# The last output weight of a feed-forward, loaded, rounded and split in two halves

## The reference, cut to what matters

```python
x = _ln(ALPHA * x + 0.5 * _swiglu(x, f_in[1], f_out[1]), g[2], b[2])   # D_MODEL 1024, D_FF 2816, 544 tokens, fp32
```

## Time and profile before

| | |
|---|---|
| median of 3 runs | 2879.94 us (2871.91 to 2883.61) |
| the profiled execution | 2882.67 us, span of its trace 2881.1 us |
| TensorE (PE) busy | 2669.0 us, 93% of the span |
| VectorE (DVE) / ScalarE (ACT) / GpSimd (POOL) busy | 1019.4 / 764.9 / 345.2 us |
| the second feed-forward's output products | 1277 to 1426 us in layer 0, 2704 to 2851 us in layer 1 |

### The profile page before, as it was taken

One profiled execution on the slowest core, in us unless ns is written; L12 is line 12 of the kernel. 1 busy time (PEld: TensorE's weight loads), 2 busy tenths in 40 slices (PEclk: granted clock), 3 DMA queues, 4 the chain that ended last, 5 costly groups with the idle time before them and its releaser, 6 DMA issues.

```text
span 2881.1 us, 49666 instructions
## 1 busy us (share of the span) xinstructions
PE 2669.0 (93%) x18108; PEld 2385.0 (83%) x18108; DVE 1019.4 (35%) x1876; ACT 764.9 (27%) x1167; POOL 345.2 (12%) x321
## 2 busy tenths in 40 slices
PE   7999999998888899999899999999988888999996
PEld 7999788896456899999899987888954568999995
DVE  2222121535553632241532211224456437222415
ACT  2222000421342332231232210014213424222313
POOL 0000000024231200013100000001242311000240
PEclk9999999997985999999999999999957859999998
DMA  3222543113421122222122234321153301222222
GB/s 138 86 86 88 155 138 110 55 61 131 139 81 58 59 74 87 87 84 90 62 88 87 87 115 146 128 90 61 46 172 112 86 33 59 88 87 87 90 81 81
DMA packets 110003, 265.86 MB, mean 92 GB/s; under 512 B 15347, under 2 KB 85138, under 8 KB 90770
## 3 DMA queue, kind: packets, MB, share of 16 engines
q1 hardware_dynamic: 99778, 233.21, 23.9%
q0 software_dynamic: 10080, 30.73, 3.3%
HBM read 258.15 MB, written 14.24 MB: 95 GB/s over the span
## 4 chain that ended last, share of the span: by engine, by line
PE 51%; issue 36%; DVE 4%; POOL 3%; DMA 1%; ACT 1%; DVEq 1%; POOLq 1%; SPq 1%; PEldq 0%; PEld 0%; ACTq 0%
PE PS L462 50%; POOL wo_lo L393 2%; POOL wi_lo L451 1%; DVEq L1429 1%; SPq L319 1%; PE PS L952 1%; DMA WO<-wo_dram 1%; POOLq L402 1%; DVE xs L1547 0%; DVE sm L1893 0%; ACT WO L1118 0%; POOLq L406 0%; DVE Z L1432 0%; DMA WI<-wi_dram 0%; DVE WO L1432 0%
## 5 line engine op out<-in xcount | busy, mean ns | idle before, releaser
L462 PE MATMUL PS<-xs,wi_hi 128*128 128x272 f32 x5376 | 1019.3, 289 | 18.5 <-DVE wi_lo L1432 16.6
L462 PE MATMUL PS<-xs,wi_lo 128*128 128x272 f32 x3088 | 899.1, 291 | 0.0
L462 PEld LDWEIGHTS PS<-xs,wi_hi 128*128 128x128 f32 x5376 | 849.5, 190 | 19.9 <-issue 19.9
L462 PEld LDWEIGHTS PS<-xs,wi_lo 128*128 128x128 f32 x3088 | 589.6, 191 | 0.0
L393 POOL TENSOR_TENSOR wo_lo<-WO,wo_hi 128x2816 fp32r<-128x2816 f32 x24 | 151.2, 6298 | 1917.1 <-ACT wo_hi L1118 1917.1
L462 PE MATMUL PS<-H,WO 128*128 128x272 f32 x1408 | 333.2, 398 | 7.8 <-DMA WO<-wo_dram 6.3
L462 PEld LDWEIGHTS PS<-H,WO 128*128 128x128 f32 x1408 | 269.8, 193 | 69.1 <-issue 13.4
L1432 DVE TENSOR_TENSOR wi_lo<-WI,wi_hi 128x2048 fp32r<-128x2048 f32 x85 | 194.8, 2292 | 365.6 <-ACT wi_hi L1118 365.6
L462 PE MATMUL PS<-wo_hi,xs 128*128 128x352 f32 x960 | 239.3, 328 | 14.5 <-DVE xs L1547 8.2
L1118 ACT ACTIVATE wi_hi<-WI 128x2048 fp32r<-128x2048 f32 x85 | 162.8, 1915 | 285.9 <-DMA WI<-wi_dram 285.9
L462 PE MATMUL PS<-h_hi,wo_hi 128*128 128x272 f32 x704 | 208.3, 296 | 24.7 <-POOL wo_lo L393 14.1
(11 more groups left out here) (201 smaller groups left out, 2998.5 us busy)
## 6 DMA issues: line engine op xcount, KB each, us to landing
WI<-wi_dram SPq DMA_DIRECT2D x100, 1024.0 KB, 4.8
WO<-wo_dram SPq DMA_DIRECT2D x44, 1408.0 KB, 6.0
M<-cmp_t_dram SPq DMA_DIRECT2D x256, 128.0 KB, 2.2
M<-slc_k_dram SPq DMA_DIRECT2D x128, 64.0 KB, 2.0
M<-slc_k_dram POOLq DMA_DIRECT2D x128, 64.0 KB, 2.3
M<-slc_v_dram SPq DMA_DIRECT2D x128, 64.0 KB, 2.0
M<-slc_v_dram POOLq DMA_DIRECT2D x128, 64.0 KB, 2.2
o_win_s_dram<-win_rows_dram POOLq DMA_DIRECT2D x2, 4064.0 KB, 4.0
```

The source lines that it names most:

```text
L462: return nc.tensor.matmul(out, lhsT, rhs, start=start, stop=stop, skip_group_check=True)
```

## The change

The last weight (slot 1 of the last pair) is taken out of the loops. SyncE waits once and issues two transfers of 128 x 1408, each with a semaphore of its own. ScalarE rounds each half by itself. VectorE, at the start of `ln` for the third norm and ahead of its first `add_half`, subtracts each half; GpSimd's loop does one weight fewer. In pass (0,1) TensorE waits for the first half ahead of block 0 and for the second ahead of block 11. The counts of the semaphores that no longer see this weight are adjusted (`NWR`, and `wo_full[1]` by one a layer).

```diff
+NWR, HALF = NCH + KD - 1, KF // 2 * P
...
-                ffn_out(l, KD + NCH)
+                with sp.Fori(0, KD // 2 - 1) as i:
+                    for p in range(2):
+                        load_wo(l, KD + NCH + 2 * i + p, p)
+                load_wo(l, NWO - 2, 0)
+                sp.wait_ge(wo_done, at(l, NWO, NWO))
+                for n in range(2):
+                    sp.dma_start(WO[:, 1, n * HALF:(n + 1) * HALF],
+                                 wo[ds(l * NWO + NWO - 1, 1), :, n * HALF:(n + 1) * HALF].rearrange("o p n -> p (o n)")
+                                 ).then_inc(end_full[n], 16)
...
-                with pool.Fori(0, KD // 2) as i:
+                with pool.Fori(0, KD // 2 - 1) as i:
                     for p in range(2):
-                        low_wo(at(l, NCH + KD, NCH + p + 1) + 2 * i, p)
+                        low_wo(at(l, NWR, NCH + p + 1) + 2 * i, p)
+                low_wo(at(l, NWR, NWR), 0)
...
-                def begin(i, p):
-                    pe.wait_ge(wo_split, at(l, NCH + KD - 2, NCH - 2 + p + 1) + 2 * i)
+                def begin(i, p, halves=False):
+                    if not halves:
+                        pe.wait_ge(wo_split, at(l, NWR - 2, NCH - 2 + p + 1) + 2 * i)
...
-                                begin(KD // 2 - 1, p)
+                                begin(KD // 2 - 1, p, p == 1)
                             for k in range(KF):
+                                if (a, p) == (0, 1) and k % (KF // 2) == 0:
+                                    pe.wait_ge(end_split, at(l, 2, k // (KF // 2) + 1))
                                 last = products(p, k, a)
...
+                square(KD // 2 - 2, 0)
+                round_wo(l, KD + NCH, 0, KD // 2 - 1)
+                square(KD // 2 - 2, 1)
+                for n in range(2):
+                    act.wait_ge(end_full[n], 16 * at(l, 1, 1))
+                    s = slice(n * HALF, (n + 1) * HALF)
+                    af(wo_hi[1][:, s], WO[:, 1, s], ACT.Copy).then_inc(end_rounded, 1)
...
                 if s == 2:
+                    for n in range(2):
+                        dve.wait_ge(end_rounded, at(l, 2, n + 1))
+                        c = slice(n * HALF, (n + 1) * HALF)
+                        tt(wo_lo[:, 1, c], WO[:, 1, c], wo_hi[1][:, c].bitcast(F32), ALU.subtract).then_inc(end_split, 1)
                     add_half(l, 2, 0, 0)
```

More of the change, by code:

```diff
@@ L261, in build @@
         wo_rounded, wo_split = sem("wo_rounded"), sem("wo_split")
+        end_full = [sem("end_full0"), sem("end_full1")]
+        end_rounded, end_split = sem("end_rounded"), sem("end_split")
         wm_rounded, wm_split = sem("wm_rounded"), sem("wm_split")
@@ L294, in ffn_in @@
                         load_wi(l, bi + 2 * i + p, p)
[L296 to L299, removed]
             def load_pages(l, first, n, src, p, width):
@@ L418, in _ @@
                     for p in range(2):
-                        low_wo(at(l, NCH + KD, p + 3) + 2 * i, p)
+                        low_wo(at(l, NWR, p + 3) + 2 * i, p)
                 pool.wait_ge(pj_freed, at(l, 30, 30 + 5))
@@ L573, in begin @@
                 def begin(i, p):
-                    pe.wait_ge(wo_full[p], 16 * (at(l, NWO // 2, bo // 2 + 1) + i))
+                    pe.wait_ge(wo_full[p], 16 * (at(l, NWO // 2 - p, bo // 2 + 1) + i))
                     pe.wait_ge(y_added, at(l, NY, y0 + p + 1) + 2 * i)
@@ L629, in chunk @@
                     else:
-                        pe.wait_ge(wo_split, at(l, NCH + KD - 2, p + 1) + 2 * (i - 1))
+                        pe.wait_ge(wo_split, at(l, NWR - 2, p + 1) + 2 * (i - 1))
                     for t in range(5):
@@ L1124, in round_wo @@
             def round_wo(l, bo, p, i):
-                act.wait_ge(wo_full[p], 16 * (at(l, NWO // 2, bo // 2 + 1) + i))
+                act.wait_ge(wo_full[p], 16 * (at(l, NWO // 2 - p, bo // 2 + 1) + i))
                 af(wo_hi[p][:, :], WO[:, p, :], ACT.Copy).then_inc(wo_rounded, 1)
@@ L1181, in squares_3, with square @@
             def squares_3(l):
-                with act.Fori(0, KD // 2 - 1) as i:
+                def square(i, p):
+                    act.wait_ge(y_added, at(l, NY, Y_AT[2] + p + 3) + 2 * i)
+                    af(sq, x[:, ds(2 * i + p, 1), :].rearrange("p o t -> p (o t)"), ACT.Square).then_inc(sq_ready, 1)
+                with act.Fori(0, KD // 2 - 2) as i:
                     for p in range(2):
-                        act.wait_ge(y_added, at(l, NY, Y_AT[2] + p + 3) + 2 * i)
-                        af(sq, x[:, ds(2 * i + p, 1), :].rearrange("p o t -> p (o t)"), ACT.Square).then_inc(sq_ready, 1)
+                        square(i, p)
                         round_wo(l, KD + NCH, p, i + 1)
+                square(KD // 2 - 2, 0)
[5 more added lines that the diff above has]
+                    af(wo_hi[1][:, s], WO[:, 1, s], ACT.Copy).then_inc(end_rounded, 1)
             def squares(l, beside):
@@ L1570, in ln @@
                 if s == 0:
-                    dve.wait_ge(wo_rounded, at(l, NCH + KD, 1))
+                    dve.wait_ge(wo_rounded, at(l, NWR, 1))
                     tt(wo_lo[:, 0, :], WO[:, 0, :], wo_hi[0][:, :].bitcast(F32), ALU.subtract).then_inc(wo_early, 1)
@@ L1577, in ln @@
                     normalise(l, 0, 1, {})
-                    dve.wait_ge(wo_rounded, at(l, NCH + KD, 2))
+                    dve.wait_ge(wo_rounded, at(l, NWR, 2))
                     tt(wo_lo[:, 1, :], WO[:, 1, :], wo_hi[1][:, :].bitcast(F32), ALU.subtract).then_inc(wo_early, 1)
```

## The result

The changed kernel takes 2861.17 us, the median of seven runs (2854.40 to 2876.07); the kernel before, run beside it, 2879.94. The ratio is 0.9941 [0.9918, 0.9965], so 10 to 24 us less, and the forecast of 2861.0 us holds. The profiled execution took 2868.56 us, with a span of 2867.1.

What follows compares the result with a forecast made beforehand. TensorE, busy 93% of the span, was bound where it waited for GpSimd's low part: 14.4 us standstill and 4.2 slow clock, together 18.7, off the median 2879.94 gives 2861 us, range 2851 to 2872.

Steps and rivals of the forecast that it cites:

- The loss before: TensorE's wait for GpSimd's low part before pass (0,1): 10.25 us in layer 0, 8.42 in layer 1, 18.7 together.
- slow-clock term: Products after that wait run at half clock: 2.77 us in layer 0, 1.47 in layer 1, 4.2 together.
- The first half's landing: SyncE's first 704 KB transfer of the last weight lands 4.2 us after issue, bounds 3.4 and 6.2.
- Rounding and low part: For each 1408-column half, ScalarE's rounding takes 1.38 us and VectorE's subtraction 1.63.
- The time to spare: At the start of (0,1), the first low half reaches TensorE 0.4 us before it is due, in each layer.
- The second half: Lands 6.2 us after the first issue, at worst 6.2 after its own; no wait at TensorE, 1.8 us spare.
- What queues behind VectorE's waits: VectorE's add of (0,0)'s output moves from 1390.17 to 1392.0, ScalarE's square likewise; pass (0,1) covers both.
- The gain is kept: Everything after (0,1) moves forward at its present distances, so the 18.7 us are kept in full.
- Rival 3: Gaps behind the change fall at other moments; further slow clock takes back 6 to 11 us: 2867 to 2872, chance 0.08.
- Rival 1: The first half lands no sooner than the whole weight did; 2.85 us are given back: 2864, chance 0.17.
- its dearer end: The clock also falls after the short waits before (0,1), costing another 4.2 us: 2868.
- Rival 2: The second half lands last, TensorE waits ahead of block 11 in (0,1), the kernel slows: 2885 to 2890, chance 0.03.

Runs made afterwards that it cites:

- one transfer: Against the changed kernel, the last weight lands in a single transfer; rounding and subtraction stay in halves on ScalarE and VectorE: 2864.18 us, ratio 0.9948.
- the subtraction earlier: Against the changed kernel, VectorE makes the next layer's first low part behind the third norm's fifth scaling; TensorE's column sums wait four blocks more: 2857.06 us.

## Why the prediction was right, point by point

- **The loss before, 10.25 and 8.42 us.** A got shorter by 10.31, B by 8.48. Both terms are borne out by the kernels that bring the wait back in part: with about 1 us of standstill and no slow clock little more than the standstill is lost, with 3 to 4 us both are. The size of the slow-clock term, 4.2 us, is that of one execution: behind other waits 12 to 26 products ran slow. That the median lies within 0.2 us of the forecast is luck, since its interval is 14 us wide.
- **The first half's landing.** Estimated 4.2 us between two rows of other sizes; measured 3.99 and 4.30, and 4.13 and 4.15 in the repeat.
- **Rounding and low part.** 1.38 and 1.63 us by scaling with the columns; the groups by line show 1382 and 1626 ns:

```profile
L1452 DVE TENSOR_TENSOR wo_lo<-WO,wo_hi 128x1408 fp32r<-128x1408 f32 x4 | 6.5, 1626 | 6.9 <-ACT wo_hi L1128 6.9
L1128 ACT ACTIVATE wo_hi<-WO 128x1408 fp32r<-128x1408 f32 x4 | 5.5, 1382 | 6.0 <-DMA WO<-wo_dram 6.0
```

- **The time to spare.** Predicted 0.4 us in each layer. Layer 0: 1392.81 + 1.63 + 0.24 = 1394.68 for a product that was due at 1395.28, 0.6 us. Layer 1: 2809.57 + 1.63 + 0.24 = 2811.44, 7.66 us after the issue against 7.95, 0.3 us. It is thin, as forecast, and the kernel with one transfer shows what missing it by a microsecond costs: about 1.3 us a layer.
- **The second half.** Expected with the whole weight's landing, 6.2 us, at the latest 6.9; measured 5.65 and 6.00, so that it had 3.2 us to spare in layer 0 rather than 1.8. The 1.8 had been worked out with the latest landing. Of all terms this was furthest off, on the safe side.
- **What queues behind VectorE's waits.** The first add moves to 1395.94, and the next one still finds VectorE idle for 6.36 us: covered, as argued.
- **The gain is kept.** From the first product of the next layer to the issue in layer 1 the two traces agree within 0.02 us. That closeness is luck: the same stretch is 1381.26 us in the repeat, and over the nine traces it runs from 1372.99 to 1385.52. Rival 3 was the right thing to fear in a single trace; the medians of the change and of its repeat show nothing of it, though an interval of 10 to 24 us alone would not rule out its smaller end.
- **The rivals.** Rival 1 would have left two waits of a microsecond and no slow clock (one transfer, 2.6 us); its dearer end, with 4.2 us more of slow clock, did not come in that kernel. Rival 2's wait, made on purpose with 12 us of landing, takes half the gain and leaves the kernel no slower than before; its working had taken a landing of 19.8 us. In the trace before, that landing is one of the 64 KB loads of another stage (`M<-slc_k_dram`), and no load of a weight took more than 11.8; the change's second halves were there 5.65 and 6.00 us after the first issue.

One question the prediction left open, and carried as the two ends of rival 1: whether a gap of some 1.5 us brings the slow clock as one of 7.5 us does. At the last weight it did not, for gaps of 0.67 to 1.24 us; what the traces say of gaps near 2 us stands below.

## What to carry to other kernels

Cut the last transfer of a chain when the consumer can start on the first part, and look at where each part stands on its queue: the second half cost nothing where it directly followed the first, and 9 us behind two other loads. A shorter wait may be worth far more, or far less, than its length, since the clock behind it is part of its price: halving the wait left the slow clock in place, and the two kernels whose waits were about a microsecond were free of it. An idle engine is not free help when its operation holds something that the busy engine needs; look at the duration of the busy engine's instructions beside it, and not only at the list of waits.

## What the runs showed of the hardware that was not expected

- **Short gaps and the clock.** After waits for the low part of 0.67, 1.24, 1.15 and 1.06 us (halves on GpSimd, one transfer) the granted clock stayed at 1.00. After those of 2.75, 2.91, 3.66, 3.82, 6.79 and 7.32 us 12 to 26 products ran at the half clock, and which of two like gaps costs more changes: 21 and 12 products behind 3.82 and 3.66 us. The length of a gap doesn't settle it, though. Near 2 us the traces show both. Where the second feed-forward waits for VectorE's low part of `h`, the clock fell for a part of the stretch behind a gap of 2.02 us in the changed kernel, and stayed at 1.00 behind one of 1.96 us in its repeat; it also stayed at 1.00 behind the 2.08 us in the kernel with the subtraction earlier. TensorE's timeline and the window behind it, in the changed kernel and then in the repeat:

```profile
1298.52 0.39 PE L469 MATMUL PS<-h_hi,wo_hi 128*128 128x272 f32 x1 [2.02 <-DVE h_lo L1452]
...
1298.50:1303.00 4.50, 4.48 (x24) 4.48 (x25) 3.39 (x4) 0.00 (x0) 0.00 (x0) 0.64 0.00 0
```
```profile
1296.95 0.39 PE L469 MATMUL PS<-h_hi,wo_hi 128*128 128x272 f32 x1 [1.96 <-DVE h_lo L1452]
...
1296.90:1301.50 4.60, 4.55 (x36) 4.55 (x37) 3.42 (x4) 0.00 (x0) 0.00 (x0) 1.00 0.00 0
```

- **Two halves land as the whole does.** The second half landed 1.66 and 1.70 us after the first, 5.65 and 6.00 after the first issue; the whole weight took 6.09 and 6.06 in layer 0 (one transfer; whole weight on VectorE). 704 KB in 1.68 us are 429 GB/s. The queue served its transfers in the order of issue here (with the second half late, the four landings in layer 0 came 4.2, 6.7, 10.4 and 12.0 us after the first issue), and the second half followed the first by less than the 4 us that a half took by itself: the transfers overlapped. By the page of the Trainium skill that the prediction cites, DMA: Bandwidth & Descriptors, section Anatomy of one DMA — SWDGE (gpsimd) path, a fit made on GpSimd's path, a half alone comes to an estimated 3.7 us, against 3.99 to 4.30 here on SyncE's queue, and its rate of 436 GB/s agrees with the 429; the 7.3 us that the second half would take if it paid its fixed part behind the first did not come.
